# Expert outputs weighted in PSUM reads, a residual add moved into the gather, and two weight blocks loaded earlier

## What is computed

```python
x = x + g1 * mix
h = modulate(x, norm2_g[layer], sh2, sc2)
x = x + g2 * moe(h, router_w, router_b, moe_w_gate[layer], moe_w_up[layer], moe_w_down[layer])
...
scores = jax.nn.sigmoid((t @ router_w).astype(jnp.float32))
...
w = w / jnp.sum(w, axis=-1, keepdims=True)
gates = jnp.sum(jax.nn.one_hot(ids, N_EXPERTS, dtype=jnp.float32) * w[..., None], axis=1).astype(h.dtype)
hid = jax.nn.silu(jnp.einsum('nd,edf->nef', t, w_gate)) * jnp.einsum('nd,edf->nef', t, w_up)
y = jnp.einsum('nef,efd->nd', hid * gates[:, :, None], w_down)
```

## Time and profile before

| | us |
|---|---|
| median of three runs | 1092.39 |
| lowest and highest run | 1092.37, 1094.45 |
| profiled execution, its own time | 1094.67 |
| its span | 1092.9 |
| TensorE busy in it | 963.6 |
| VectorE, ScalarE, GpSimd busy | 356.7, 204.1, 141.9 |

### The profile page before, as it was taken

How to read it: one execution, slowest core, us unless ns; L and a number is a source line. 1 busy time by engine, 2 the same in 40 slices (tenths; PEclk the granted TensorE clock), 3 DMA queues, 4 the chain that set the end, 5 groups by cost and what they waited for, 6 DMA issues and landing times.

```text
span 1092.9 us, 14325 instructions
## 1 busy us (share of the span) xinstructions
PE 963.6 (88%) x5748; PEld 492.2 (45%) x5748; DVE 356.7 (33%) x838; ACT 204.1 (19%) x416; POOL 141.9 (13%) x152
## 2 busy tenths in 40 slices
PE   2799999998889995999997299999999959999970
PEld 1555445576555554433332144444655544333320
DVE  0201420015644655411111441420346564111116
ACT  4211100015641110111111440000210101111112
POOL 4000140003750001001000400100000010010002
PEclk9799999998999995999999599999999959999995
DMA  9979658875242004999992943200340049999927
GB/s 338 377 251 357 223 195 289 324 274 159 74 160 102 37 22 149 414 391 423 415 414 85 338 162 106 77 0 1 92 169 39 20 153 414 378 425 420 421 84 285
DMA packets 86246, 247.39 MB, mean 226 GB/s; under 512 B 7472, under 2 KB 21456, under 8 KB 73760
## 3 DMA queue, kind: packets, MB, share of 16 engines
q1 hardware_dynamic: 58960, 202.72, 48.4%
q0 software_dynamic: 8960, 29.57, 7.2%
q10 hardware_dynamic: 18256, 14.14, 4.2%
HBM read 217.24 MB, written 28.38 MB: 225 GB/s over the span
## 4 chain that ended last, share of the span: by engine, by line
PE 83%; DMA 7%; DVE 5%; issue 2%; ACT 2%; POOL 0%; SPq 0%; DVEq 0%; ACTq 0%; POOLq 0%
PE bank L1670 24%; PE bank L1778 17%; PE bank L1682 13%; PE bank L1792 8%; DMA ring<-in_ada_w 4%; PE bank L1640 4%; PE bank L1626 3%; PE bank L1769 3%; DMA ring<-in_sg_w_in 2%; PE bank L1695 1%; PE bank L1936 1%; PE bank L2011 1%; DMA uv<-y_rows,small 1%; PE bank L1928 1%; PE bank L2058 1%
## 5 line engine op out<-in xcount | busy, mean ns | idle before, releaser
L1670 PE MATMUL bank<-ring,h_feat 128*128 128x512 f32 x640 | 283.0, 600 | 6.5 <-DMA ring<-in_sg_w_in 5.8
L1778 PE MATMUL bank<-ring,uv 128*32 128x512 f32 (+2 forms) x640 | 188.9, 603 | 2.2 <-ACT uv L928 2.2
L1670 PEld LDWEIGHTS bank<-ring,h_feat 128*128 128x128 f32 x640 | 121.1, 192 | 154.9 <-issue 153.9
L1682 PE MATMUL bank<-ring,h_feat 128*128 128x512 f32 x320 | 148.3, 615 | 0.0
L1778 PEld LDWEIGHTS bank<-ring,uv 128*32 128x32 f32 (+2 forms) x640 | 59.8, 134 | 92.9 <-issue 87.9
L1792 PE MATMUL bank<-ring,uv 128*32 128x512 f32 (+2 forms) x320 | 94.2, 595 | 1.3 <-ACT uv L951 1.3
L1682 PEld LDWEIGHTS bank<-ring,h_feat 128*128 128x128 f32 x320 | 60.5, 196 | 67.6 <-issue 67.4
L1409 DVE TENSOR_TENSOR uv<-uv,bank 128x256 f32<-128x256 f32 x26 | 11.0, 421 | 163.9 <-ACT uv L943 163.9
L1626 PE MATMUL bank<-small,h_tok 128*128 128x128 f32 x224 | 35.5, 307 | 31.3 <-ACT h_tok L1093 20.5
L1640 PE MATMUL bank<-ring,small 128*2 128x128 f32 x1152 | 39.4, 293 | 24.5 <-DMA ring<-in_ada_w 24.5
L817 POOL DMA_INDIRECT uv<-h_rows,small x26 | 24.7, 949 | 223.7 <-PE bank L1769 193.0
(11 more groups left out here) (211 smaller groups left out, 1004.4 us busy)
## 6 DMA issues: line engine op xcount, KB each, us to landing
ring<-in_ada_w SPq DMA_DIRECT2D x16, 2048.0 KB, 14.6
ring<-in_moe_w_gate SPq DMA_DIRECT2D x20, 1024.0 KB, 13.1
ring<-in_moe_w_up SPq DMA_DIRECT2D x20, 1024.0 KB, 15.2
ring<-in_moe_w_down SPq DMA_DIRECT2D x20, 1024.0 KB, 14.9
y_rows<-uv SPq DMA_DIRECT2D x26, 512.0 KB, 9.1
h_tok<-in_moe_w_down SPq DMA_DIRECT2D x12, 1024.0 KB, 13.8
ring<-in_na_w_in SPq DMA_DIRECT2D x4, 2048.0 KB, 16.1
bz<-in_ada_w SPq DMA_DIRECT2D x4, 2048.0 KB, 12.0
```

The lines of the kernel that those rows point to most:

```text
L1670: last = mm(jbank(key)[:, :], HT[:, cc, P * t:P * (t + 1)], w[:, cc, :], start=cc == 0, stop=cc == DC - 1)
L1682: last = mm(jbank(key)[:, :], HT[:, cc, P * t:P * (t + 1)], blk_ap(("out", layer, b))[:, cc, :], start=cc == 0, stop=cc == DC - 1)
L1778: last = mm(bank[2][32 * q:32 * (q + n), :], XT[:, b, cc, 32 * q:32 * (q + n)], w[:, :, cc, :], start=cc == 0, stop=cc == DC - 1)
```

## The change

1. VectorE reads both halves of the down products and weights them on the way, by the row's routing weight (`row_w`) and by a row of g2 (`row_gate`, made anew for each pass); ScalarE no longer reads them. The weights per row come from the late tables, whose products grow from 12 to 37 columns. g2 is broadcast in pass 0 on ScalarE's queue instead of later on SyncE's.
2. The first gather of a tile adds its rows to X in the transfer; the second writes to `picked_rows`, and VectorE adds that to X. The weighting by ScalarE and two of VectorE's three steps per tile go.
3. With an empty overflow, the blocks 2 and 3 of layer 1's input projection are loaded behind passes 10 and 11 of layer 0, block 2 at RING[6144:10240]; block 0 when the last tile's gathers have landed, block 1 after block 2 has been used.
4. For the last tile of the routing the logits come ahead of the scaling of H and `pick` ahead of its last add.
5. After layer 0, ScalarE's and VectorE's steps stand in another order, and GpSimd takes the first tile's power ahead of the last tile's gathers.
6. Overflow passes on VectorE are written out instead of looped.

```diff
-LOADS += [(("in", 1, b), b) for b in (2, 3, 0, 1)] + [(("out", 1, b), 2 + b) for b in range(2)]
+EARLY_IN = 6
+LOADS += [(("in", 1, 2), EARLY_IN)] + [(("in", 1, b), b) for b in (3, 0, 1)] + [(("out", 1, b), 2 + b) for b in range(2)]
...
-        late_oh = late(2 * TT * MAXOV).rearrange("p (k n) -> p k n", n=MAXOV)
+        late_oh = late(2 * TT * (NTILE + MAXOV)).rearrange("p (k n) -> p k n", n=NTILE + MAXOV)
...
-                sp.wait_ge(x_mid, 2 * TT * (layer + 1))
-                for q in range(2):
-                    sp.dma_start(g_b[:, q, :], mod(layer, q, 5).to_broadcast([P, D])).then_inc(bcast_g_in, 16)
-
...
                 for e in range(FIRST_OVERFLOW, NPASS):
                     refill(e)
+                    for o, b in ((0, 2), (1, 3)):
+                        if layer == 0 and LAST_PASS[OVERFLOW_AFTER[o]] == e:
+                            with sp.If(n_over < 1):
+                                load_block(("in", 1, b), sgin_v[b])
...
-                    for b in (2, 3, 1, 0):
-                        if b == 2:
-
-                            sp.wait_ge(got[0], 32)
-                        if b == 3:
-                            sp.wait_ge(got[TT - 1], 32)
-                        load_block(("in", 1, b), sgin_v[b])
...
+                    sp.wait_ge(got[TT - 1], 32)
+                    load_block(("in", 1, 0), sgin_v[0])
+                    wait_job(sp, ("p", 1, 2, TT - 1))
+                    load_block(("in", 1, 1), sgin_v[1])
...
                 for t in range(TT):
...
+                    if layer == 0 and t == TT - 1:
+                        rstd_of(2 * TT)
+                    nc.gpsimd.indirect_dma_start(
+                        out=X[:, t, :], out_offset=None, in_=y_rows[:, :],
+                        in_offset=bass.IndirectOffsetOnAxis(ap=slot_i[:, t, 0:1], axis=0), compute_op=ALU.add)\
+                        .then_inc(got[t], 16)
+                    nc.gpsimd.indirect_dma_start(
+                        out=picked_rows(t), out_offset=None, in_=y_rows[:, :],
+                        in_offset=bass.IndirectOffsetOnAxis(ap=slot_i[:, t, 1:2], axis=0)).then_inc(got[t], 16)
...
+                    if e == 0:
+                        for q in range(2):
+                            act.dma_start(g_b[:, q, :], mod(layer, q, 5).to_broadcast([P, D])).then_inc(bcast_g_in, 16)
...
-            scale_first(0, 0)
-            scale_first(0, 1)
+            norm_squares(0)
             norm_rows(0)
-            scale_first(0, 2)
+            norm_squares(1)
             read_tile(1, ("tt", 0, 0), 0)
             norm_rows(1)
-            scale_first(0, 3)
+            norm_squares(2)
+            read_tile(1, ("tt", 1, 0), 1)
             norm_rows(2)
-            scale_first(0, 4)
+            norm_squares(3)
             gelu(2, 0)
-            read_tile(1, ("tt", 1, 0), 1)
             read_tile(1, ("tt", 2, 0), 2)
             norm_rows(3)
+            norm_squares(4)
...
                     dve.wait_ge(rstd, k + 1)
+                    if t == TT - 1:
+                        logits(t)
                     link(nc.vector.scalar_tensor_tensor(H[:, t, :], X[:, t, :], rs[:, t:t + 1], sc_b[:, cnd(t), :],
                                                         ALU.mult, ALU.mult))
                     if t == TT - 1:
-                        logits(t)
+                        pick(t)
                     nc.vector.tensor_tensor(H[:, t, :], H[:, t, :], sh_b[:, cnd(t), :], ALU.add).then_inc(h2_ready, 1)
-                pick(TT - 1)
...
+                weights, over = late_oh[:, :, 0:NTILE], late_oh[:, :, NTILE:]
+                tt(late_tiles, bc(hi, NTILE), row(tile_lo, 2 * TT), ALU.is_equal)
+                tt(weights, late_tiles, bc(w12.rearrange("p s t -> p (s t)"), NTILE), ALU.mult)
...
+            def row_tables(layer):
+
+                dve.wait_ge(late_idx_mm, layer + 1)
...
+                dve.wait_ge(bcast_g_in, 32 * (layer + 1))
+                tt(g_b[:, 0, :], g_b[:, 0, :], g_b[:, 1, :], ALU.subtract)
+
+            def weigh(tile, b, left, right):
+
+                nc.vector.scalar_tensor_tensor(YO[:, b, 0:512], bank[5][:, :], row_w[:, tile:tile + 1],
+                                               row_gate[:, 0:512], ALU.mult, ALU.mult).then_inc(left, 1)
+                nc.vector.scalar_tensor_tensor(YO[:, b, 512:1024], bank[6][:, :], row_w[:, tile:tile + 1],
+                                               row_gate[:, 512:1024], ALU.mult, ALU.mult).then_inc(right, 1)
+
+            def gate_rows(tile):
+
+                return nc.vector.scalar_tensor_tensor(row_gate, g_b[:, 0, :], row_prompt[:, tile:tile + 1],
+                                                      g_b[:, 1, :], ALU.mult, ALU.add)
...
                 def read_y(e, b, round_):
+                    if e:
+                        dve.wait_ge(y_right, base + e)
+                    link(gate_rows(e))
                     if round_ is not None:
 
                         dve.wait_ge(y_stored[b], 16 * (rounds(b) * layer + round_))
                     dve.wait_ge(down_mm, base + e + 1)
-                    nc.vector.tensor_copy(YO[:, b, 512:1024], bank[6][:, :]).then_inc(y_dve, 1)
+                    weigh(e, b, y_left, y_right)
...
-                dve.wait_ge(g_scaled, TT * layer + t + 1)
-                link(nc.vector.scalar_tensor_tensor(y1, y2, w12[:, 1, t:t + 1], y1, ALU.mult, ALU.add))
-                scaled = nc.vector.tensor_tensor(y2, y1, g_b[:, cnd(t), :], ALU.mult)
-                link(scaled)
-                nc.vector.tensor_tensor(X[:, t, :], X[:, t, :], y2, ALU.add).then_inc(x_out, 1)
+                dve.wait_ge(got[t], 32 * (layer + 1))
+                nc.vector.tensor_tensor(X[:, t, :], X[:, t, :], picked_rows(t), ALU.add).then_inc(x_out, 1)
...
-            for t in range(TT):
+            combine(0, 0)
+            mean_square(2 * TT)
+            combine(0, 1)
+            read_tile(1, ("tt", 0, 1), 0)
+            mean_square(2 * TT + 1)
+            for t in range(2, TT):
                 combine(0, t)
                 mean_square(2 * TT + t)
-                if t:
-                    read_tile(1, ("tt", t - 1, 1), t - 1)
+                read_tile(1, ("tt", t - 1, 1), t - 1)
...
-                        pe.wait_ge(y_act, base + e)
-                        pe.wait_ge(y_dve, base + e)
+                        pe.wait_ge(y_left, base + e)
+                        pe.wait_ge(y_right, base + e)
```

More of the change, by code:

```diff
@@ L523, in build @@
         for key, s in LOADS:
-            landed[s] += 2 if s == SPLIT or key == ("dft",) else 1
-            place[key] = (s, landed[s])
+            i = signal_of(s)
+            landed[i] += 2 if s == SPLIT or key == ("dft",) else 1
+            place[key] = (s, landed[i])
         def wait_block(eng, key):
             s, n = place[key]
-            eng.wait_ge(block_in[s], 16 * n)
+            eng.wait_ge(block_in[signal_of(s)], 16 * n)
         def blk_ap(key):
@@ L802, in _ @@
                 if layer == 1:
-                    for t in range(TT):
+                    for t in range(1, TT):
                         rstd_of(2 * TT + t)
@@ L931, in experts @@
                 base = NPASS * layer
-                def read_y(e, b, round_):
-                    if round_ is not None:
-                        act.wait_ge(y_stored[b], 16 * (rounds(b) * layer + round_))
-                    act.wait_ge(down_mm, base + e + 1)
-                    nc.scalar.activation(YO[:, b, 0:512], bank[5][:, :], ACT.Copy).then_inc(y_act, 1)
                 def body(e, b, round_, round_before):
@@ L1137, in _ @@
             experts(1)
-            for t in range(TT):
-                scale_first(1, t)
         @blk.vector
@@ L1435, in experts @@
                     read_xt_over(1, 1)
-                with dve.Fori(0, MAXOV // 3) as g:
-                    for u in range(3):
-                        o, s = 3 * g + u, (u + 1) % 3
-                        with dve.If(n_over > o):
-                            dve.wait_ge(o_["silu"], o + 1)
-                            nc.vector.tensor_tensor(hid, silu_g, bank[2][:, FF:2 * FF], ALU.mult)\
-                                .then_inc(o_["hid"], 1)
-                            with dve.If(n_over > o + 1):
-                                read_xt_over(o + 2, (s + 1) % 3)
-                            dve.wait_ge(y_stored[s], 16 * rounds(s) * (layer + 1))
-                            dve.wait_ge(o_[f"stored{s}"], g + 1)
-                            dve.wait_ge(o_["down_mm"], o + 1)
-                            nc.vector.tensor_copy(YO[:, s, 512:1024], bank[6][:, :]).then_inc(o_["y_dve"], 1)
@@ L1451, in combine @@
-            def combine(layer, t):
-                dve.wait_ge(bcast_g_in, 32 * (layer + 1))
-                y1, y2 = picked_rows(t)[:, 0, :], picked_rows(t)[:, 1, :]
-                dve.wait_ge(g_scaled, TT * layer + t + 1)
-                link(nc.vector.scalar_tensor_tensor(y1, y2, w12[:, 1, t:t + 1], y1, ALU.mult, ALU.add))
```

(19 more changed lines are left out.)

81 lines of the change are left out of this document (36 added, 45 removed).

## The result

Over 13 runs of each kernel the median went from 1093.14 to 1100.68 us: a ratio of 1.0062, 95% interval 1.0049 to 1.0075. The forecast was 1088.9 and its range ended at 1097.0. The change makes the kernel slower, by 5.4 to 8.2 us at the ends of that interval.

What follows compares the result with a forecast made beforehand. The prediction took weight loads between the layers, VectorE at the end and TensorE inside the passes to bound the kernel. Terms 1.6 + 0.5 - 1.6 - 4.0 = -3.5 us gave a median of 1088.9, range 1085.3 to 1097.0.

Steps and rivals of the forecast that it cites:

- the floor: Tail gathers of layer 1: an add in the transfer costs nothing more per gather than a plain one.
- the ceiling: Adding gathers: at most another 512 KB at 396 GB/s, 1.32 us more per gather.
- the sign: Tail of layer 1: the forecast falls if the last landing comes 25 us after the first gather.
- full second read: Mainly the tail: the residual's read adds all of 1.32 us to each adding gather; slower, 1096.1 us; chance 0.23.
- The early load of block 3: End of layer 0: block queued ahead of the last two row stores delays the last by 0.5 us, bounds 0 and 1.5.
- First gather to second projection: After layer 0: first projection starts at 15.4 us, second ends at 40.9 after the first gather instead of 42.5; -1.6 us.
- Weighting on VectorE: Last pass of each layer: down products wait 0.55 us longer and the last weighting ends 0.75 us later than the copy.
- Wider late tables: Late-index tables of each layer: two larger mask steps and 37-column products cost +0.5 us.
- Picking earlier: Last routing tile of each layer: picking before the last add saves 1.0 us; 2 us of cover remain for store and gather.
- After the last landing: End of layer 1: one add, then the 3.07 us behind it, from 21.25 to 25.65 us after the first gather.
- Half of it hidden: Tail and transition: 0.74 us of the residual's read is left per tile; sum +0.5, 1092.9 us; chance 0.25.
- the clock holds: Gap before layer 1's second projection: clock doesn't fall, projection takes 7.1 us, 2.4 more gained, 1086.5 us; chance 0.10.

Runs made afterwards that it cites:

- the order run: Changed kernel with ScalarE's first gelu ahead of tile 3's squares and tile 1 read behind it, adding gathers kept; median 1091.95 us, ratio 0.9985 to before.

## Why the prediction was wrong

**The failed step** is "I take the floor, as the nearest row is the plain gather of the same rows on the same queue". The floor held for the plain gathers (21.56 us to the last landing, 21.25 forecast); the adding gather costs 1.28 us more, and 27.94 is 0.1 over what the floor and five times the ceiling of 1.32 give. The prediction had named the sign itself: it falls if the last landing comes 25 us after the first gather. The end took 32.18 us instead of 25.65, 6.5 of the 10.4 us between the sum of -3.5 and the table's +6.9. The row that should have decided was in the rival's own argument: engines 0.95 busy with gathers alone. With the engines full, the extra work cost nearly its ceiling here. I chose by the likeness of the operation instead of by the load of the resource. The Trainium skill, DMA: Bandwidth & Descriptors, section Anatomy of one DMA, gives bytes over 436 GB/s for the movement of a transfer. If the second read counts as bytes, the estimate from it is 1.2 us, which agrees with the 1.16 to 1.38 measured here; that the extra time is a read of the residual is not shown by any run, only its size.

**The rival "full second read"** had the place and the size (6.6 forecast at the end, 6.4 measured), and its mechanism fits them. Its 1096.1 is still low by 4.6: 3.2 are other terms that were short, 0.75 is that the kernel before came out at 1093.14 and not at 1092.39, and the rest lies between profiles and medians. The terms:

- *The early load of block 3*: +0.5 with bounds 0 to 1.5; the store took 5.26 instead of 3.04, +2.2, beyond the bound. I let the store wait out the rest of the block's time at the full rate, with nothing else counted; undone, the store took 2.65. That the early block is the cause is shown by that run; whether by the order of one queue or by full engines, no run separates. The Trainium skill, DMA: Bandwidth & Descriptors, section Queues, rings and completion order, says that each engine takes a ring's descriptors in order; the late store agrees with it.
- *First gather to second projection*: 40.9 forecast, 42.4 measured, 42.5 before. The gap (6.7, measured 6.62), the table load as its last part, the half clock behind it (9.41, measured 9.53) and its cause all stand, the last shown by the order run. The start was off: 17.6 instead of 15.4, and this is a second step that failed, "GpSimd issues the first eight gathers, 1.25 us apart". That is the pace of plain gathers. An adding one takes GpSimd 1.55 us instead of 0.94, so the eighth gather was out 12.2 us after the first issue instead of 9.95, and the power of tile 0, on the same engine, ended at 12.9 instead of 10.5. The first tile's rows were late too (8.24 instead of 6.4), but their squares and mean (L1148) were ready 1.4 us before GpSimd was free (rows below the list). A faster first projection (8.59) gave 0.8 back.
- *Weighting on VectorE*: +0.55 and +0.75 forecast, +0.7 and +0.75 measured, per layer. *Wider late tables*: +0.5 forecast, +0.57 and +0.58 by the chain (0.29 of it the longer products); the rest of that stretch's +0.66 and +0.80 is the first 16 gate and up products, 9.75 and 9.98 us instead of 9.63 and 9.74.
- *Picking earlier*: -1.0, measured -1.09 in both layers. No store or gather behind it was late.
- *After the last landing*: 4.4 forecast, 4.24 measured, one add per tile started by a landing.

The start of the hand-over in the changed kernel, the mean of tile 0 on VectorE, then the eighth gather and the power on GpSimd:

```profile
611.29 0.15 DVE L1148 TENSOR_SCALAR small<-small 128x1 f32<-128x1 f32 x1 [1.21 <-ACT ps L869]
...
611.89 0.96 POOL L857 DMA_INDIRECT uv<-y_rows,small  x1 [0.30 <-issue]
612.88 0.60 POOL L764 TENSOR_TENSOR small<-small 128x1 f32<-128x1 f32 x1
```

"Half of it hidden" and "the clock holds" fall: 1.28 is near the whole, and in both profiles of the change the granted clock was 0.50 in the first 4 us behind the gap.

That the first profile came out only 1.3 us longer in span than the one before was chance: without the table by stretches it would have looked like +0.1%.

## What to carry to other kernels

Before an operation moves into a transfer, look at the busy share of the transfer engines at that very place: where they were full here, it cost 1.2 to 1.4 us of 512 KB there and 0.6 us more on the queue that issues it, even if the engine it leaves was the one that bound. When one wait goes, read which in-order queue releases the next step (here ScalarE's gelu behind squares that weren't ready); moving a few calls gave back 6 to 8 us, while the add in the transfer lost time. And compare profiles stretch by stretch between the same events, since two executions of one program differ by several us in stretches that no edit touched.

## What was not expected of the hardware

- An adding gather of 512 KB takes the transfer engines 1.16 to 1.38 us longer than a plain one, and GpSimd 1.55 us to issue instead of 0.94.
- With TensorE busy throughout, its granted clock falls to half for part of a stretch and comes back, at different places in executions of the same program; 16 products then take 8.64 instead of 6.95 us. From the long run of projections to layer 1's router this made 219.07, 220.77 or 222.46 us, steps of 1.7.
- A 2 MB weight load took 20.52 us beside gathers of which half add, and 16.80 beside plain ones; in the change, where none of these loads runs beside gathers, three of them landed in 7.9 to 9.7.
